# A hybrid attention and DeltaNet step on one core: heads attended in pairs, V products laid out by token

## What is computed

```python
# B: a block of 128 queries of a latent head reads up to 3 blocks of keys, 256 context keys and a sink
l_loc = where(mask, einsum('bkgqd,bksd->bkgqs', qi, ki) * scale, NEG_INF)
l_ctx = einsum('bkgqd,bkpd->bkgqp', qi, ck) * scale
p = softmax(concatenate([l_loc, l_ctx, sk], -1), -1)
out = einsum('bkgqs,bksd->bkgqd', p[..., :span], vi) + einsum('bkgqp,bkpd->bkgqd', p[..., span:-1], cv)
# C: the same without a sink; a table of relative positions is added to the local logits
l_loc = einsum('bhqd,bhrkd->bhqrk', qr, kr) * scale + bias
l_loc = where(col_mask, l_loc, NEG_INF)
# context tokens read only context tokens: softmax(q k^T * scale (, sink)) v
```

## Time and profile before

| | us |
|---|---|
| median of 3 runs | 2798.97 (2798.52 to 2800.76) |
| the profiled execution's own time | 2799.91 |
| its span | 2798.0 |
| PE busy in the span | 2472.2 (88%) |
| DVE busy | 1619.8 (58%) |
| ACT busy | 1086.8 (39%) |
| mean granted clock of TensorE | 0.916 |

### The profile page before, as it was taken

The page is one execution under the profiler, slowest core; times in us unless marked ns, Lnnn a source line. Parts: engine busy times, 40 slices in busy tenths (PEclk is TensorE's granted clock), DMA queues, the critical chain, the costliest instruction groups (busy, mean ns, idle before and its releaser), DMA issues.

```text
span 2798.0 us, 52168 instructions
## 1 busy us (share of the span) xinstructions
PE 2472.2 (88%) x22710; PEld 1563.7 (56%) x22710; DVE 1619.8 (58%) x2632; ACT 1086.8 (39%) x1380; POOL 72.2 (3%) x70
## 2 busy tenths in 40 slices
PE   7699988849888999999889998968986999998994
PEld 4356678836544555555446668855645444444442
DVE  0354734546644455453265634537734999998886
ACT  0233412225513222220033431224513788887774
POOL 0000000000000000000000000000000100110001
PEclk9899968968998999999989978977996999999997
DMA  9511010010111222123711000010003999999896
GB/s 338 200 61 47 17 39 3 4 63 1 45 62 62 90 91 76 61 76 130 277 53 52 27 8 34 4 63 1 1 1 147 402 404 408 408 404 369 342 359 228
DMA packets 58291, 381.43 MB, mean 136 GB/s; under 512 B 7280, under 2 KB 8304, under 8 KB 16592
## 3 DMA queue, kind: packets, MB, share of 16 engines
q1 hardware_dynamic: 50160, 346.38, 32.2%
q0 software_dynamic: 7904, 31.72, 3.1%
HBM read 362.61 MB, written 15.47 MB: 135 GB/s over the span
## 4 chain that ended last, share of the span: by engine, by line
PE 39%; DVE 6%; ACT 2%; DVEq 1%; issue 1%; DMA 1%; PEldq 0%; PEld 0%; ACTq 0%; POOL 0%
PE ps L1773 6%; PE ps L1747 4%; PE ps L1749 4%; PE ps L1748 4%; PE ps L146 2%; PE ps L147 2%; PE ps L148 2%; PE ps L1324 2%; PE ps L1310 1%; PE ps L1340 1%; PE ps L1109 1%; PE ps L1107 1%; PE ps L1529 1%; PE ps L1668 1%; PE ps L1313 1%
## 5 line engine op out<-in xcount | busy, mean ns | idle before, releaser
L146 PE MATMUL ps<-scan,work 128*128 128x512 f16 (+1 forms) x1024 | 285.3, 302 | 61.7 <-DVEq L269 37.0
L147 PE MATMUL ps<-scan,work 128*128 128x512 f16 (+1 forms) x1024 | 286.2, 302 | 0.0
L148 PE MATMUL ps<-scan,work 128*128 128x512 f16 (+1 forms) x1024 | 282.7, 302 | 0.0
L247 ACT ACTIVATE work<-ring 128x2048 f16<-128x2048 f32 x52 | 98.2, 1903 | 332.2 <-DVEq L183 213.4
L301 PE MATMUL ps<-ring,work 128*48 128x256 f32 x768 | 171.1, 387 | 18.5 <-DMA ring<-in_wmod 16.0
L146 PEld LDWEIGHTS ps<-scan,work 128*128 128x128 f16 x1024 | 100.8, 98 | 129.3 <-issue 66.0
L146 PE MATMUL ps<-pj,scan 128*128 128x128 f16 (+1 forms) x544 | 150.9, 301 | 24.5 <-DVEq L269 18.5
L1731 DVE SCALAR_TENSOR_TENSOR work<-ring,work 128x2048 f16<-128x2048 f32 x68 | 154.1, 2287 | 21.3 <-ACT work L1727 21.3
L1731 DVE SCALAR_TENSOR_TENSOR scan<-ring,scan 128x2048 f16<-128x2048 f32 x68 | 155.4, 2287 | 8.4 <-ACT scan L1727 8.4
L1731 DVE SCALAR_TENSOR_TENSOR pj<-hT,pj 128x2048 f16<-128x2048 f32 x68 | 152.5, 2284 | 6.9 <-ACT pj L1727 6.9
L1458 DVE SCALAR_TENSOR_TENSOR xT<-ps,mod,xT 128x128 f32<-128x128 f32 x208 | 100.4, 543 | 93.9 <-PE ps L148 93.9
(11 more groups left out here) (399 smaller groups left out, 5817.0 us busy)
## 6 DMA issues: line engine op xcount, KB each, us to landing
ring<-in_e SPq DMA_DIRECT2D x136, 1024.0 KB, 8.5
hT<-in_e SPq DMA_DIRECT2D x68, 1024.0 KB, 8.2
ring<-in_wmod SPq DMA_DIRECT2D x48, 1024.0 KB, 4.9
ring<-in_d SPq DMA_DIRECT2D x33, 1024.0 KB, 5.0
ring<-in_win SPq DMA_DIRECT2D x24, 1024.0 KB, 4.9
yslots<-pj POOLq DMA_DIRECT2D x17, 512.0 KB, 8.7
ring<-in_wout SPq DMA_DIRECT2D x8, 1024.0 KB, 8.5
ring<-in_wv SPq DMA_DIRECT2D x4, 1024.0 KB, 4.8
```

Source lines behind the costliest of these rows:

```text
L146: nc.tensor.matmul(out, w[0], x[0], start=start, stop=False)
L147: nc.tensor.matmul(out, w[0], x[1], start=False, stop=False)
L148: return nc.tensor.matmul(out, w[1], x[0], start=False, stop=stop)
```

## The change

1. Attention goes by pairs of heads. The two heads of a pair lie in opposite halves of the array's rows (features on partitions 0 to 63 and 64 to 127): heads i and i+2 in B, heads 2i and 2i+1 in C. `pair_scores_pe` makes the local scores of both heads (banks 0 and 1), then the context scores of both (banks 2 and 3). DVE handles the logits of both heads in one instruction each (`logits_dve`), with the maximum and its negative for both.
2. The V product is turned round (`pv_pe`): the transposed probabilities (128 x 128) are stationary, and 64 columns of V stream. The result has tokens on partitions.
3. DVE's pass that divides the row is gone. ACT divides while it copies the V product out of PSUM (`output`), with the reciprocal as a scale per partition, into a 128 x 128 buffer `osb` that holds both heads of the pair. PE then transposes that buffer (`joined_pe`, into a part of bank 3), and DVE copies it to `hT`.
4. Buffers: four for the logits (`lbufs`), four for the transposed probabilities (in `scr`).
5. The position table is masked in the DeltaNet: `rpb_mask` takes 512 columns at a time, eight pieces of the product in wave 1 and eight of the sum in wave 2, behind each step of DVE.

```diff
@@ gdn_all_dve @@
                     if w < NW:
                         gdn_dve(dve, l, w, i, False)
+                    if w == 1 and i == 0:
+                        dve.wait_ge(S["rpb_loaded"], 16 * (l + 1))
+                    if w in (1, 2):
+                        rpb_mask(w, i)
@@ PE, attention @@
+        def pair_scores_pe(pe, l, i):
+            x = PAIRS[i]
+            if i:
+                pe.wait_ge(S["lg_read"], l * NPR + i)
+            at, kv = slice(x["t"] * P, x["t"] * P + P), slice(x["loc"][0] * P, (x["loc"][-1] + 1) * P)
+            for p, h in enumerate(HALVES):
+                mm = nc.tensor.matmul(bank(p)[:, 0:x["nl"]], pj[h, x["q"], at], pj[h, x["k"], kv], start=True, stop=True)
+            if x["ctx"]:
+                for p, h in enumerate(HALVES):
+                    mm = nc.tensor.matmul(bank(2 + p)[:, 0:PAST], pj[h, x["q"], at], ck[h, x["c"], :], start=True, stop=True)
...
-                mm = nc.tensor.matmul(bank(6 + u % 2)[x["hs"], 0:P], v, ptbuf(u)[:, j * P:(j + 1) * P],
+                mm = nc.tensor.matmul(bank(6 + u % 2)[:, 0:L], ptbuf(u)[:, j * P:(j + 1) * P], v,
...
+        def joined_pe(pe, l, i):
+            if not 0 <= i < NPR:
+                return
+            pe.wait_ge(S["o_ready"], l * NU + 2 * i + 2)
+            pe.wait_ge(S["lg_read"], l * NPR + min(i + 4, NPR))
+            if i:
+                pe.wait_ge(S["ot_free"], l * NPR + i)
+            nc.tensor.transpose(bank(3)[:, PAST:PAST + P], osb(i), ident[:, :]).then_inc(S["ot_ready"], 1)
...
+            pair_scores_pe(pe, l, 0)
+            for i in range(NPR + 3):
+                joined_pe(pe, l, i - 3)
+                if i + 1 < NPR:
+                    pair_scores_pe(pe, l, i + 1)
+                probs_pe(pe, l, 2 * i - 1)
+                pv_pe(pe, l, 2 * i - 3)
+                pv_pe(pe, l, 2 * i - 2)
+                probs_pe(pe, l, 2 * i)
@@ DVE, attention @@
-                nc.vector.tensor_scalar(lbuf(u)[:, 0:n], lbuf(u)[:, 0:n], att[:, a + 2:a + 3], None,
-                                        ALU.mult).then_inc(S["pn_ready"], 1)
+            for i in range(NPR + 4):
+                if i < NPR:
+                    dve.wait_ge(S["sc_ready"], l * NPR + i + 1)
+                if i >= 4:
+                    x = PAIRS[i - 4]
+                    dve.wait_ge(S["ot_ready"], l * NPR + i - 3)
+                    nc.vector.tensor_copy(hT[:, x["o"], x["t"] * P:(x["t"] + 1) * P],
+                                          bank(3)[:, PAST:PAST + P]).then_inc(S["ot_free"], 1)
+                if i < NPR:
+                    logits_dve(dve, l, i)
+                if 1 <= i <= NPR:
+                    dve.wait_ge(S["p_ready"], l * NU + 2 * i)
+                    a = 8 + 2 * ((i - 1) % 2)
+                    nc.vector.reciprocal(att_rec(i - 1), att[:, a:a + 2]).then_inc(S["r_ready"], 1)
@@ ACT, attention @@
+                    act.wait_ge(S["pv_ready"], l * NU + u + 1)
+                    act.wait_ge(S["r_ready"], l * NPR + u // 2 + 1)
+                    nc.scalar.activation(osb(u // 2)[:, L * (u % 2):L * (u % 2) + L], bank(6 + u % 2)[:, 0:L], ACT.Identity,
+                                         bias=par[:, l, C_ZERO:C_ZERO + 1],
+                                         scale=att_rec(u // 2)[:, u % 2:u % 2 + 1]).then_inc(S["o_ready"], 1)
+            for i in range(NPR + 2):
+                exp(2 * i)
+                copy(2 * i - 1)
+                exp(2 * i + 1)
+                copy(2 * i)
+                output(2 * i - 3)
+                output(2 * i - 2)
```

More of the change, by code:

```diff
@@ L1298, in lbuf @@
         def lbuf(u):
[L1299 removed]
+            return lbufs[:, u % 4, :]
         def ptbuf(u):
[L1302 to L1314 removed]
@@ L1316, in attn_pv, with osb @@
[L1316 to L1322 removed]
+            return scr[:, (u % 4) * 768:(u % 4) * 768 + 768]
+        def osb(i):
+            return scr[:, 3072 + P * (i % 2):3072 + P * (i % 2) + P]
@@ new lines, in probs_pe, with pv_pe @@
+        def probs_pe(pe, l, u):
+            if not 0 <= u < NU:
+                return
+            pe.wait_ge(S["p_ready"], l * NU + u + 1)
+            if u:
+                pe.wait_ge(S["pt_copied"], l * NU + u)
+            for j in range(PAIRS[u // 2]["n"] // P):
+                mm = nc.tensor.transpose(ps[:, 4 * 512 + j * P:4 * 512 + (j + 1) * P], lbuf(u)[:, j * P:(j + 1) * P], ident[:, :])
+            mm.then_inc(S["pt_ready"], 1)
+        def pv_pe(pe, l, u):
+            if not 0 <= u < NU:
+                return
+            x = PAIRS[u // 2]
+            pe.wait_ge(S["pt_copied"], l * NU + u + 1)
+            if u >= 2:
+                pe.wait_ge(S["o_ready"], l * NU + u - 1)
+            vc = x["vc"][u % 2]
+            vs = [vtok[:, t, vc:vc + L] for t in x["loc"]] + [cv[:, j, vc:vc + L] for j in range(x["ctx"])]
```

184 lines of the change are left out of this document (71 added, 113 removed).

## The result

| | before | after |
|---|---|---|
| median, us | 2799.86 | 2773.11 (4 runs, 2768.49 to 2776.76) |
| ratio | 1 | 0.9903, 95% interval 0.9887 to 0.9919 |
| the profiled execution's own time, us | 2799.91 | 2776.76 |
| its span, us | 2798.0 | 2774.9 |
| mean granted clock | 0.916 | 0.915 |

The change makes the kernel 27 us faster. I forecast 60 us slower, and the range began at 2808, so the prediction was wrong in sign.

The account below looks back on a forecast made before the run. PE was taken to bound attention, but for its start. Per layer 167.6 for attention plus 2.4 for masks less 140.2 gave +29.8, over two layers +59.6, so 2859 us; range 2808 to 2905.

Parts of the forecast that it names:

- The clock: Attention: the clock rises late and falls again at times; 40% of the 87.6 us gap, giving 167.6 us a layer.
- my two sums: A layer's attention from its first scores: 132.6 us at 2.4 GHz throughout, 220.2 us at 1.2 GHz.
- a sign of being wrong: Attention's windows: a mean clock of 0.85 or more would show the prediction wrong; below 0.85, right.
- the hole: Before the joined transpose PE waits for ACT's scaled copy, once a pair: 1.14 us, bounds 0 and 1.5.
- the rival with the clock at 0.50 all through: Attention stays at 1.2 GHz throughout: 220.2 us, +82.4 a layer, 2964 us; chance 0.05.
- The first rival: Attention's clock rises where it did before and holds: 147.5 us, +9.7 a layer, 2818 us; chance 0.23.
- Scores: Attention, six-tile pair: the two heads' halves overlap in part, 2.0 us instead of 2.98; bounds 1.5 and 3.0.
- The V products: Attention: twelve instructions, bound by 128-column loads, take 1.5 us against 1.46 before; lower bound 0.8.
- the rival with streamed columns: V products go by streamed columns, loads hidden: 128 us a layer, -9.8, 2779 us; chance 0.12.
- The sum: Attention, six-tile pair at 2.4 GHz: PE's terms add to 8.1 us, 1.1 more than before.
- The masks: DeltaNet: two mask pieces in each of two waves delay PE, 2.4 us a layer; bounds 0 and 9.6.
- the main case: Attention with the wait before the joined transpose, load-bound V products and both clock levels: 2859 us; chance 0.57.

Follow-up runs that it names:

- head-by-head run: The changed kernel with a pair's scores issued one head after the other (local and context of one, then of the other), not in turns: 2777.29 us, ratio 0.9917.
- the early copies: ACT's two scaled copies put before its copy of the second unit's transposes: 2734.74 us on the changed kernel, 2939.76 us with all scores also in the lower half.

## Why the prediction was wrong, step by step

Four of the runs form a table that holds most of the answer (us):

| | scores in one half | in both halves |
|---|---|---|
| V products by feature, no joined transpose, no division | 2776.6 | 2713.4 |
| V products by token, joined transpose, scaled copy (the change) | 2976.2 | 2773.1 |

Using both halves for the scores is worth 63 us in the upper row and 203 in the lower. V products by token cost 60 us with paired scores and 200 without. The change puts a loss of 60 and a gain of 63 or more together; the upper left kernel, whose PE work is nearly that of before, is 24 us faster than before, by the pairs on DVE and ACT, the missing division and the masks together; no run takes these apart, but for the masks, which alone gained 13.

**The clock: the step that failed.** I put attention at 1.2 GHz for 40% of the gap between my two sums, 35 us a layer. In the changed kernel attention is at 0.50 for 16.6 us of 117.4 in the first layer, and for 31.2 of 124.9 in the second, with a relapse of 3.4 us behind that. Its mean of 0.93 and 0.86 lies above the 0.85 that I had named as a sign of being wrong. I gave two grounds. The first, the hole, is refuted: with the hole the changed kernel holds 1.00 through its steady part, and without the hole one half stays at 0.50. The second, that products bound by 128-column loads and streaming little do not keep the clock, is borne out where the scores use one half: 0.50 throughout with 64 streamed columns, a mean of 0.82 with 128, and at clock 1.00 an instruction's duration differs by only 2 ns. What I left out is the other side of the change. Two heads' scores in two halves stand against it, and with them the clock rose after 17 us in the first layer and 31 in the second. Without them the rival with the clock at 0.50 all through (2964) would have come about: 2976. So the mechanism was right for the V products, and the prediction forgot to ask the same question of the scores. The first rival (the clock rises where it did and holds) is the one that came true in kind, though the clock rose earlier than it did before; it was priced at 2818 for the sizes below.

**Scores: mis-sized.** 2.0 us forecast for a six-tile pair, 1.49 measured, my lower bound. I let the second head's first pass start beside the first head's second pass; both start within 7 ns of each other (695.966 and 695.973) and go side by side to the end. Eight six-tile, four five-tile and four four-tile pairs make it some 7 us a layer.

**The V products: right in kind, 15% too high.** 3.0 us forecast for two of twelve instructions, 2.62 measured, 109 ns an instruction where I took the router's 126. Loads bind them, which 128 streamed columns at the same duration show; the rival with streamed columns is refuted (its threshold was 1.15 us for one product, and one takes 1.31), though its 2779 is the number nearest to the result. That it lies only 6 us away is an accident.

**The hole: right.** 1.14 us forecast, 1.20 behind six tiles and 1.09 behind five measured, released by ACT's scaled copy; the scaled copy alone takes 0.40 busy, not 0.24, within the bounds. Taking it away gave 38 us, 1.2 for each of 32 pairs.

**The sum.** With 1.49 for the scores, 2.62 for the V products, 0.72 for the first transposes and the rest as forecast, a six-tile pair comes to 0.26 + 1.49 + 0.72 + 2.62 + 0.88 + 1.20 = 7.2 us at clock 1.00, not 8.1. In proportion that is about 13 us less a layer for the sixteen pairs. For the one-tile pairs and the filling I took 15; the changed kernel issues the fifth pair's scores 8.5 us after the first's, though at clock 0.50, and the pipeline's end is longer than the 2 us that I gave it, 16.6 us from the start of the last scores to the end of the last joined transpose, most of which the pairs' own sums hold already. So my sum at 2.4 GHz, 132.6, was too high even for what the chip did with 16.6 us at the low clock, 117.4. Without the 35 us for the clock my own terms give 132.6 + 2.4 - 140.2 = -5.2 a layer, so 2789: the clock alone turned the sign. Measured, attention is 22 and 15 us a layer shorter and the stretch ahead of it 8 longer, which is 22 of the profiled executions' 23 us.

How much of the 22 and 15 is the clock can be estimated from PE's busy time at 0.50. Before, it was 31.3 and 31.7 us of the time until the rise, as these windows show:

```profile
612.07:652.80 40.73, 31.26 (x87) 18.71 (x88) 28.08 (x77) 12.94 (x45) 0.00 (x0) 0.50 0.00 0
1888.12:1929.30 41.18, 31.72 (x89) 18.84 (x89) 28.46 (x78) 13.40 (x45) 0.00 (x0) 0.50 0.00 1
```

In the changed kernel it was 14.0 and, with the relapse, 30.0. If that work takes half the time at 1.00, the earlier rise gave about 9 us in the first layer and 1 in the second, and some 14 us in each come from the rest, up to 8.2 of them from the start that no longer waits for the masks and is paid back in the DeltaNet. By this estimate the turn with its pairs and its hole is worth only some 6 us a layer.

**The masks: direct cost right, the loss of clock left out.** I forecast 2.4 us a layer. Where the clock held in waves 1 and 2 they grew by 1.4 and 1.2, as these windows of the second layer of the head-by-head run show:

```profile
1705.19:1739.17 33.98, 29.89 (x881) 29.29 (x878) 22.32 (x61) 7.89 (x18) 0.00 (x0) 1.00 0.02 4
1739.17:1771.79 32.62, 28.44 (x838) 27.82 (x836) 22.23 (x60) 7.89 (x18) 0.00 (x0) 1.00 0.02 4
```

(before, the second layer's were 32.56 and 31.42). In the changed kernel the clock also fell once, briefly, in each of the two waves (a mean of 0.95), and stood at 0.50 for other lengths of time at the DeltaNet's two ends, so that it was 8 us a layer there. In that layer of the other run DVE's first product and the first scores lie 209.3 us apart, in the changed kernel 217.0, with the same code in between. I had called the DeltaNet's clock safe, because it stayed at 1.00 before; the spare was small, and I didn't cost its loss. My bounds of 0 to 9.6 hold both values.

**Transposes, and the swap of operands.** The Trainium skill, TensorE: Matmul & The Clock Gate, Part 4, says that transposes don't engage the full clock. The traces disagree for these f32 transposes. In the kernel before, PE runs nothing but 28 transposes behind the 80 matmuls of the router:

```profile
2133.79 5.08 PE L1545 MATMUL ps<-ident,hT 128*128 128x128 f32 x28
```

The clock, at 0.50 through the 80 matmuls, rises at 2137.6 us, inside these transposes, and it rises inside them in the profile of every kernel of this document. The changed kernel's clock also stands at 1.00 with 1.5 us of transposes in a turn of 6.68. The Trainium skill, TensorEngine Tiling (Array Packing), Performance Considerations, advises to swap operands where 64 columns would be streamed and to use both column halves. The runs agree in direction: 60 us are lost by giving the swap up, 21 of which remain after the hole is gone, though the kernels with the swap leave the division out. I used the advice for the main case and gave too little weight to the row tiling that stands in the same section, which is what the paired scores are.

What stays open: whether it is the second half's work that raises the clock, or that the scores take less of PE's time when they run side by side; no run separates the two. And how the clock chooses its moment. Between two layers with the same code it rose 16.6 and 31.2 us after the first scores. These differences move a time by up to 8 us, so that gains of that size (the streamed columns in the changed kernel, the masks alone) are seen in the runs but not explained to the last part. No run computes the division with V products by feature in pairs, so the price of DVE's division there was not measured, and the 60 us between the kernels without and with it hold for a kernel that doesn't divide.

## What to carry to other kernels

When a change alters how much of the array works at a time, judge the clock by all of PE's kinds of work together, those that it improves too, before costing a part of the time at the low clock: here the same V products ran at 0.50 or at 1.00 depending on whether the scores beside them used one half or two. Look at an in-order engine's program for an early result that stands behind late work; one call moved behind two others was worth more (38 us) than the whole change (27 us). Put filler work where the engine waits in the tail of a pipeline, not evenly into waves whose partner has no time to spare: moved there, the masks gave 7 us in one kernel and 11 in the other.

## What the runs showed of the hardware

- The two row halves of the array each follow their own order. Issued behind two matmuls (four passes) of the lower half, the upper half's first pass started 13 ns after the lower half's first, as read from the spacing of the passes.
- Two 64x128 f32 products in the two row halves take what one takes (1.49 us for a six-tile pair and for one six-tile head). Two in the same half take 2.78, 0.2 less than twice.
- In a V product with 128x128 f32 stationary operands an instruction takes 109 ns at clock 1.00 with 64 streamed columns, and 2 ns more with 128.
- With V products by token and scores in one half, PE busy for 99% of 178 us was at 1.2 GHz throughout (with the early copies). In the same kernel without the early copies, streaming 64 more columns per V product, whose results nobody reads, saved 141 us.
- 64-column stationary operands in the two column halves overlap even when they belong to two products issued one after the other: 24 instructions in 2.39 us, 100 ns each on average, against 122 for one product alone.
- 28 f32 transposes of 128x128 in a row, with no other work of PE, stood over the rise of the clock from 1.2 to 2.4 GHz in the router (at 2137.6 in the kernel before, and in every other profile).
